# An mLSTM and dilated attention block: the chunk products as fp32r matmuls of high and low parts, with the state as a pair

## What is computed

```python
def step(carry, inp):
    C, n, m = carry
    k_j, v_j, a_j, bt_j = inp
    m_new = jnp.maximum(bt_j + m, a_j.max(-1))
    decay = jnp.exp(bt_j + m - m_new)
    w = jnp.exp(a_j - m_new[..., None])
    C_new = decay[..., None, None] * C + jnp.einsum('bhl,bhlk,bhlv->bhkv', w, k_j, v_j)
    n_new = decay[..., None] * n + jnp.einsum('bhl,bhlk->bhk', w, k_j)
    return (C_new, n_new, m_new), (C, n, m)
...
s = jnp.einsum('bhnld,bhnsd->bhnls', qc, kc) * jnp.exp(log_d - m_t[..., None])
num = inter[..., None] * jnp.einsum('bhnld,bhndv->bhnlv', qc, C_prev) + jnp.einsum('bhnls,bhnsv->bhnlv', s, vc)
den = inter * jnp.einsum('bhnld,bhnd->bhnl', qc, n_prev) + s.sum(-1)
h = num / jnp.maximum(jnp.abs(den), jnp.exp(-m_t))[..., None]
```

## Time and profile before

| | us |
|---|---|
| median of 3 runs | 1372.53 (1372.0 to 1373.92) |
| the profiled execution, its own time | 1374.74 |
| its span, first to last instruction | 1372.9 |
| busy in the span: PE / DVE / ACT / POOL | 1352.4 / 792.1 / 642.1 / 568.1 |
| PE's chain share of the span | 89% |
| granted PE clock, mean | 0.996 of 2.4 GHz |

### The profile page before, as it was taken

How to read it: one execution, slowest core, us unless ns; L and a number is a source line. 1 busy time by engine, 2 the same in 40 slices (tenths; PEclk the granted TensorE clock), 3 DMA queues, 4 the chain that set the end, 5 groups by cost and what they waited for, 6 DMA issues and landing times.

```text
span 1372.9 us, 18735 instructions
## 1 busy us (share of the span) xinstructions
PE 1352.4 (99%) x6448; PEld 1126.6 (82%) x6448; DVE 792.1 (58%) x1261; ACT 642.1 (47%) x1320; POOL 568.1 (41%) x399
## 2 busy tenths in 40 slices
PE   7999999999999999999999999999999999999998
PEld 4788888888888888888888888888888888788786
DVE  4864338245543835877657675755644442897632
ACT  5644543553454455445545455444544553533421
POOL 3353435335443534664434445344343554454000
PEclk8999999999999999999999999999999999999999
DMA  6123233324333232454442635345343354966421
...
DMA packets 210462, 165.02 MB, mean 120 GB/s; under 512 B 32400, under 2 KB 186544, under 8 KB 210368
## 3 DMA queue, kind: packets, MB, share of 16 engines
...
...
q10 hardware_dynamic: 432, 0.10, 0.0%
...
## 4 chain that ended last, share of the span: by engine, by line
PE 89%; DVE 4%; DMA 2%; issue 2%; ACT 2%; SPq 1%; POOL 0%; ACTq 0%; DVEq 0%; POOLq 0%
PE proj L1240 68%; PE side L1185 3%; PE proj L1185 2%; PE side L1285 2%; PE side L1264 2%; PE side L1341 2%; PE side L1350 2%; PE side L1273 1%; PE side L1313 1%; PE side L1346 1%; DMA hm_raw_T<-hm_spill 1%; PE proj L1166 1%; PE side L1166 1%; PE side L1296 1%; PE side L1358 1%
## 5 line engine op out<-in xcount | busy, mean ns | idle before, releaser
L1075 POOL TENSOR_TENSOR w_lo<-raw,w_hi 128x512 fp32r<-128x512 f32 x161 | 233.3, 1450 | 410.7 <-ACT w_hi L1449 410.7
L1240 PE MATMUL proj<-hi_T,w_hi 128*128 128x512 f32 x832 | 338.2, 406 | 2.3 <-ACT snap L1467 1.6
L1240 PE MATMUL proj<-hi_T,w_lo 128*128 128x512 f32 x832 | 325.2, 391 | 0.0
L1240 PE MATMUL proj<-lo_T,w_hi 128*128 128x512 f32 x832 | 324.1, 390 | 0.0
L1240 PE MATMUL proj<-hi_B,w_hi 128*128 128x512 f32 x624 | 255.0, 409 | 5.5 <-ACT b_sb L1511 5.5
L1240 PE MATMUL proj<-hi_B,w_lo 128*128 128x512 f32 x624 | 245.0, 393 | 0.0
L1240 PE MATMUL proj<-lo_B,w_hi 128*128 128x512 f32 x624 | 244.6, 392 | 0.0
L1075 POOL TENSOR_TENSOR w_lo<-s_sb,w_hi 128x512 fp32r<-128x512 f32 x104 | 157.0, 1513 | 156.9 <-ACT w_hi L1449 156.8
L1240 PEld LDWEIGHTS proj<-hi_T,w_hi 128*128 128x128 f32 x832 | 156.4, 188 | 36.3 <-issue 3.7
L1240 PEld LDWEIGHTS proj<-hi_T,w_lo 128*128 128x128 f32 x832 | 156.1, 188 | 34.2
L1240 PEld LDWEIGHTS proj<-lo_T,w_hi 128*128 128x128 f32 x832 | 156.6, 188 | 30.3
...
## 6 DMA issues: line engine op xcount, KB each, us to landing
...
```

The lines of the kernel that those rows point to most:

```text
L1075: TT(w_lo_ring[k % RING][:], src, w_hi_ring[k % RING][:].bitcast(F32), ALU.subtract).then_inc(lo_pool, 1)
L1240: mm = pe.matmul(acc(p, which), w[:, kt, :], m[:, kt, :], start=(first and kt == 0 and w is wh and m is h_hi[b]), stop=(kt == 3 and w is w ...
```

## The change

The scores stay as they are. All other products of the chunks become three fp32r matmuls each, of a high and a low part (`three_products`). That needs:

- on ACT, vv and kw written as fp32r high parts (vv_hi, kw_hi), and a new copy q_hi of the chunk's q (not in a head's first chunk);
- on DVE, at a chunk's start: vv_lo and kw_lo from PSUM less the high parts, ahead of the product of scores and mask, which now goes in place into dmat; a cast cw_hi and a subtraction cw_lo of it; and q_lo, which is written over q in the chunk's buffer;
- on DVE, at a chunk's end: the state as a pair state_hi and state_lo. The two halves from PSUM are added to the decayed state_lo into state_sum, then the decayed state_hi is added (128x516), and the sum is cast into state_hi and the rest written into state_lo;
- single buffers for vv, kw, w and the gate of o, where there were two. ACT waits for the last product of the chunk before (L1715 before: of the one two back), and the gate's tanh for the gating of the chunk before;
- PE's end of a chunk waits for kv_done (now DVE's), q_low, st_done and w_done;
- apart from this, the second load of x counts on the semaphore of the first one (x_in) in place of one of its own.

```diff
@@ -470,11 +470,17 @@
             pos[0] += (int(np.prod(shape[1:])) * size + 31) // 32 * 32
             return t
 
-        state = small("state", [P, 2, VE], F32)
-        kw_sb = [small(f"kw{i}", [P, MD], F32) for i in range(2)]
-        vv_sb = [small(f"vv{i}", [P, VE], F32) for i in range(2)]
-        w_sb = [small(f"w{i}", [P, P], F32) for i in range(2)]
-        o_gate = [small(f"o_gate{i}", [P, MD], F32) for i in range(2)]
+
+        state_hi = small("state_hi", [P, 2, VE], F32R)
+        state_sum = small("state_sum", [P, 2, VE], F32)
+
+        state_lo = at("state_lo", [P, 2, VE], F32R, pos[0] - (2 * VE * 4 + 31) // 32 * 32)
+        q_hi = at("q_hi", [P, 2, P], F32R, A_P + 26112)
+        q_lo = [at(f"q_lo{i}", [P, 2, P], F32R, A_P + 16896 + i * 4608) for i in range(2)]
+        kw_hi, kw_lo = small("kw_hi", [P, MD], F32R), small("kw_lo", [P, MD], F32R)
+        vv_hi, vv_lo = small("vv_hi", [P, VE], F32R), small("vv_lo", [P, VE], F32R)
+        cw_hi, cw_lo = small("cw_hi", [P, P], F32R), small("cw_lo", [P, P], F32R)
+        o_gate = small("o_gate", [P, MD], F32)
         dmat = small("dmat", [P, P], F32)
         total = small("total", [P, VE], F32)
         sq_junk = small("sq_junk", [P, MD], BF16, 2)
...
@@ -1330,25 +1338,33 @@
                     mm = pe.transpose(keep[:, MD + d * P:MD + (d + 1) * P], cb_[:, 4 + d, :], ident[:])
                 mm.then_inc(pe_keep, 1)
 
+            def three_products(into, w, m):
+
+                for i, (a, b) in enumerate(((0, 0), (0, 1), (1, 0))):
+                    mm = pe.matmul(into, w[a], m[b], start=(i == 0), stop=(i == 2))
+                return mm
+
             def chunk_end(h, n):
                 c = chunk_no(h, n)
-                v = vv_sb[c % 2][:]
+                v = (vv_hi[:], vv_lo[:])
                 pe.wait_ge(kv_done, c + 1)
                 pe.wait_ge(ones_done, 1)
                 if n:
-                    ring_taken(pe, ("C", h, n - 1, 1))
+                    pe.wait_ge(q_low, later_no(h, n))
+                    pe.wait_ge(st_done, later_no(h, n))
                     for d in range(2):
-                        mm = pe.matmul(keep[:, 0:VE], chunk_sb[c % 2][:, d, :], state[:, d, :],
-                                       start=(d == 0), stop=(d == 1))
+                        for a, m in ((q_hi, state_hi), (q_hi, state_lo), (q_lo[c % 2], state_hi)):
+                            mm = pe.matmul(keep[:, 0:VE], a[:, d, :], m[:, d, :], start=(d == 0 and a is q_hi and m is state_hi),
+                                           stop=(d == 1 and a is not q_hi))
                     mm.then_inc(pe_keep, 1)
-                ring_taken(pe, ("qk", h, n))
+                pe.wait_ge(w_done, c + 1)
                 b = work(("B", h, n))
-                pe.matmul(b[:, 0:VE], w_sb[c % 2][:], v, start=True, stop=True).then_inc(pe_ring, 1)
+                three_products(b[:, 0:VE], (cw_hi[:], cw_lo[:]), v).then_inc(pe_ring, 1)
                 if n < NT - 1:
                     for d in range(2):
                         b = work(("C", h, n, d))
-                        pe.matmul(b[:, 0:VE], kw_sb[c % 2][:, d * P:(d + 1) * P], v, start=True, stop=True
-                                  ).then_inc(pe_ring, 1)
+                        keys = slice(d * P, (d + 1) * P)
+                        three_products(b[:, 0:VE], (kw_hi[:, keys], kw_lo[:, keys]), v).then_inc(pe_ring, 1)
 
             def head_output(h, f):
                 d, j2 = f // 2, f % 2
@@ -1711,18 +1727,25 @@
                             act.wait_ge(cols_exp, 1)
                             act.wait_ge(att_out, 16 * AH)
                         act.wait_ge(pe_keep, keep_no["kv", h, n] + 1)
-                        if c > 1:
-                            act.wait_ge(pe_ring, ring_no[last_use(*divmod(c - 2, NT))] + 1)
-                        ins = A(vv_sb[c % 2][:, 0:MD], keep[:, MD:2 * MD], ACT.Copy)
+                        if c:
+                            act.wait_ge(pe_ring, ring_no[last_use(*divmod(c - 1, NT))] + 1)
+                        ins = A(vv_hi[:, 0:MD], keep[:, MD:2 * MD], ACT.Copy)
                         if n < NT - 1:
-                            ins = A(kw_sb[c % 2][:], keep[:, 0:MD], ACT.Copy, scale=cols[:, 2, h, n:n + 1])
-                        ins.then_inc(kv_done, 1)
+                            ins = A(kw_hi[:], keep[:, 0:MD], ACT.Copy, scale=cols[:, 2, h, n:n + 1])
+                        ins.then_inc(kv_hi, 1)
+                        if n:
+
+                            if later_no(h, n) > 1:
+                                hp, n2 = (h, n - 1) if n > 1 else (h - 1, NT - 1)
+                                act.wait_ge(pe_keep, keep_no["A", hp, n2] + 1)
+                            act.wait_ge(chunk_in[c % 2], 32 * (c // 2 + 1))
+                            A(q_hi[:], chunk_sb[c % 2][:, 0:2, :], ACT.Copy).then_inc(q_high, 1)
                         act.wait_ge(d_done, c + 1)
                         A(dmat[:], dmat[:], ACT.Exp, bias=cols[:, 0, h, n:n + 1]).then_inc(e_done, 1)
                         act.wait_ge(pe_ring, ring_no["oT", h, n] + 1)
-                        if c > 1:
-                            act.wait_ge(chunk_ready, c - 1)
-                        A(o_gate[c % 2][:], bank[ring_no["oT", h, n] % BANKS][:, 0:MD], ACT.Tanh, scale=0.5
+                        if c:
+                            act.wait_ge(chunk_ready, c)
+                        A(o_gate[:], bank[ring_no["oT", h, n] % BANKS][:, 0:MD], ACT.Tanh, scale=0.5
                           ).then_inc(ring_act, 1)
                     elif what == "end":
                         h, n = it[1:]
@@ -2151,18 +2174,29 @@
                 if c == 0:
                     dve.wait_ge(att_out, 16 * AH)
                     dve.wait_ge(dec_in, 16)
-                    step(V.memset(vv_sb[0][:, MD:VE], 1.0))
-                    V.memset(vv_sb[1][:, MD:VE], 1.0).then_inc(ones_done, 1)
+                    step(V.memset(vv_hi[:, MD:VE].bitcast(F32), 1.0))
+                    V.memset(vv_lo[:, MD:VE].bitcast(F32), 0.0).then_inc(ones_done, 1)
                 else:
-                    ring_taken(dve, ("qk", *divmod(c - 1, NT)))
+                    dve.wait_ge(w_done, c)
                 dve.wait_ge(chunk_in[c % 2], 32 * (c // 2 + 1))
                 TT(dmat[:], neg_g[c % 2][:], tril[:], ALU.add).then_inc(d_done, 1)
+                dve.wait_ge(kv_hi, c + 1)
+                ins = TT(vv_lo[:, 0:MD], keep[:, MD:2 * MD], vv_hi[:, 0:MD].bitcast(F32), ALU.subtract)
+                if n < NT - 1:
+                    ins = STT(kw_lo[:], keep[:, 0:MD], cols[:, 2, h, n:n + 1], kw_hi[:].bitcast(F32), ALU.mult, ALU.subtract)
+                ins.then_inc(kv_done, 1)
                 i = ring_no["qk", h, n]
                 dve.wait_ge(pe_ring, i + 1)
-                if c > 1:
-                    dve.wait_ge(pe_ring, ring_no["B", (c - 2) // NT, (c - 2) % NT] + 1)
                 dve.wait_ge(e_done, c + 1)
-                TT(w_sb[c % 2][:], bank[i % BANKS][:, 0:P], dmat[:], ALU.mult).then_inc(ring_dve, 1)
+                TT(dmat[:], bank[i % BANKS][:, 0:P], dmat[:], ALU.mult).then_inc(ring_dve, 1)
+                ring_taken(dve, ("qk", h, n))
+                if c:
+                    dve.wait_ge(pe_ring, ring_no["B", *divmod(c - 1, NT)] + 1)
+                step(V.tensor_copy(cw_hi[:], dmat[:]))
+                TT(cw_lo[:], dmat[:], cw_hi[:].bitcast(F32), ALU.subtract).then_inc(w_done, 1)
+                if n:
+                    dve.wait_ge(q_high, later_no(h, n))
+                    TT(q_lo[c % 2][:], chunk_sb[c % 2][:, 0:2, :], q_hi[:].bitcast(F32), ALU.subtract).then_inc(q_low, 1)
 
             def chunk_end(h, n):
                 c = chunk_no(h, n)
@@ -2180,17 +2214,25 @@
                 if c >= HM_SLOTS:
                     hp, n2 = divmod(c - HM_SLOTS, NT)
                     dve.wait_ge(pe_ring, ring_no["hmT", hp, 2 + n2 // 4] + 1)
-                STT(hm_slot(h, n), o_gate[c % 2][:], 1.0, total[:, 0:MD], ALU.add, ALU.mult).then_inc(chunk_ready, 1)
+                STT(hm_slot(h, n), o_gate[:], 1.0, total[:, 0:MD], ALU.add, ALU.mult).then_inc(chunk_ready, 1)
                 if n < NT - 1:
+                    if chunk_no(h, n) - h:
+                        dve.wait_ge(st_done, chunk_no(h, n) - h)
                     for d in range(2):
                         i = ring_no["C", h, n, d]
                         dve.wait_ge(pe_ring, i + 1)
                         part = bank[i % BANKS][:, 0:VE]
                         if n:
-                            STT(state[:, d, :], state[:, d, :], decay[:, h, n:n + 1], part, ALU.mult, ALU.add
+                            STT(state_sum[:, d, :], state_lo[:, d, :].bitcast(F32), decay[:, h, n:n + 1], part, ALU.mult, ALU.add
                                 ).then_inc(ring_dve, 1)
                         else:
-                            V.tensor_copy(state[:, d, :], part).then_inc(ring_dve, 1)
```

(9 more changed lines are left out.)

8 lines of the change are left out of this document (5 added, 3 removed).

## The result

| | before | after |
|---|---|---|
| median of 4 runs each, us | 1373.22 (1372.0 to 1374.43) | 1397.78 (1396.55 to 1398.89) |
| ratio, 95% interval | | 1.0176 [1.0164, 1.0187] |
| the profiled execution, its span, us | 1372.9 | 1394.8 |
| granted PE clock, mean | 0.996 | 0.993 |

A forecast was written before the change was run, and what follows sets the result against it. PE was taken to bound the kernel, busy for 437.0 of 437.0 us in the chunks. -10.4 us on PE and +15.5 of waits for DVE made +5.1, so 1377.5 us on the median, range 1363 to 1387.

The forecast's parts named there:

- PE's part: Chunks' products on PE: 432 fp32r matmuls at 0.121 us replace 288 fp32 instructions at 0.2175; 10.4 us less.
- Rival 4: On PE, weight loads don't hide behind matmuls of 258 columns and set the pace: some 1405 us; chance 0.03.
- The mechanism: DVE's added work makes PE wait for q_lo and at turns of o, in heads 0 to 2, none in head 3.
- the term of 15.5 us for DVE's delay: PE's waits on late DVE work in the heads' chunks, added to the forecast as 15.5 us.
- The prediction's own walk: DVE's and ACT's queues followed instruction by instruction; PE waits 17 us in four places in heads 0 to 2.
- a reason that no row shows: For taking 15.5 us rather than 17: a first wait of PE also spaces the rows behind it.
- start group: DVE's additions at a chunk's start (vv_lo, kw_lo, cast and subtraction for cw, q_lo), charged 0.3 us for POOL.
- end group: DVE's additions at a chunk's end (128x516 update, cast, subtraction for the state pair), charged 0.3 us for POOL.
- the charge for POOL: DVE instructions reading two SBUF tensors are held by POOL: 0.3 us per new group of a chunk, between 0 and 0.5.
- the prediction's own four sums: PE's waits: 11.6 us without POOL's charge, 17 with 0.3, 23.4 with 0.5, 22 with slow cast and 0.3.
- the slow cast: DVE's state cast at its upper end of 0.65 us instead of 0.30; with POOL's 0.3, PE waits 22 us.
- Rival 3: Worse contention: DVE holds POOL, weights come late, the cast is slow; waits of 26 us or more, from 1388; chance 0.05.

The follow-up runs named there:

- no_qlo: The changed kernel without DVE's q_lo; PE makes the same 432 matmuls with q_hi in its place, low part of q left out: 1384.75 us, 1.0078 of the kernel before.
- state_one: The changed kernel without the state's low part, state_hi updated straight from PSUM, q_lo kept, 432 matmuls kept: 1370.04 us, 0.9976 of the kernel before.
- after_notaps: The changed kernel with two of the convolution's three taps left out on DVE: 1369.02 us, 0.9967 of the kernel before; that kernel without these taps took 1373.05.

## Why the prediction was right, and where it went wrong

**PE's part was right.** 0.1195 us per matmul against 0.121, 11.0 us against 10.4. Rival 4, a weight load that sets the pace, did not come: there is one load and one matmul every 0.12 us. The Trainium skill, "TensorE: Matmul & The Clock Gate", under what overlaps and what doesn't, says that a load overlaps a matmul only in another row group. The trace does not agree with it at 258 columns either.

**The mechanism was right.** PE waits for q_lo, and at the turn of o, and in head 3's time only 1.0 us, for another instruction of DVE. Chunks 1 and 2 lose a little over 5 us where 3.8 were walked, and 1.7 of these are the clock. The split was off: 1.94 us for q_lo and 0.93 for the turn of o, where 1.1 and 2.5 were walked. DVE's busy time in the stretch came to 385.21 (380 to 395 forecast). PE waits for neither POOL nor SP there, and for ACT 1.4 us for `total` and 1.1 for snap.

**The step that failed is the term of 15.5 us for DVE's delay.** By PE's rows 28.6 us of waiting stand in its place, and 5.1 us of slow clock for which the sum had no term; by the medians 35.6 were lost. The prediction's own walk summed to 17, and was taken down to 15.5 for a reason that no row shows. Its parts:

| | predicted | measured |
|---|---|---|
| POOL's hold and slower pieces, start group, us per chunk | 0.3 | 0.87 |
| POOL's hold, end group (without the cast) | 0.3 | 0.16 |
| cast of the state, us each | 0.30 | 0.43 least, 0.50 mean |
| losses in head 0 | 8.9 | 10.3 |
| in head 1 | 3.1 | 11.7 |
| in head 2 | 5.3 | 12.0 |
| clock at 1.2 GHz | 0 | 5.1 (1.7 in each of these) |

Without the clock head 0 lost 8.6 us, as walked; heads 1 and 2 lost 10.0 and 10.3 and not 3.1 and 5.3. There five of seven q_lo are held, in head 0 three.

*First, the charge for POOL.* It was put at 0.3 us in the middle of a range up to 0.5, and it was 0.87 for the start's group: q_lo (1159 ns, 0.42 by itself) 0.74 and cw_lo (414, 0.29) 0.13. The step that gave it was wrong in kind. It took the mean hold of the gating as that of any instruction, as if POOL's work fell anywhere. But the place of a new instruction in the queue fixes what it meets: 19 of 28 q_lo met a w_lo for nearly its whole length. An estimate from the prediction's own four sums (11.6, 17 and 23.4 us for a charge of 0, 0.3 and 0.5, and 5 more for the slow cast) makes some 27 us of the measured prices, a mean charge of 0.52 and a cast of 0.50. That is near the 28.6 measured. But it is not the whole answer. In no_qlo, with q_lo and its hold both gone, those sums would give under 14.5 us, and PE is idle for 15.2 with 3.4 of slow clock on top. So the walk itself reads low too, and how the loss parts between the charge and the walk's small slack in heads 1 and 2 stays open. The experiments give the price of a crowded queue directly: taking away 32 us of DVE's busy time (no_qlo) gives back 13, some 56 (state_one) 28, some 42 (after_notaps) 29, that is 0.4 to 0.7 us for each us. The mean idle time of 165 us in the earlier trace rows told nothing of that.

*Second, a term for the clock was missing.* The forecast has PE's gaps at 1 to 3 us and nothing of what follows them. Behind three of them the clock costs 5.1 us more.

Waits and clock together are 33.7 us by PE's rows. The 35.6 of the medians are some 2 us more; that lies within what separates a profiled execution from a median here, and was not followed. The cast took 0.43 us by itself and 0.50 in the mean, between its two ends of 0.30 and 0.65. The cycle table of the Trainium skill, "VectorE: DVE Perf Modes", would make it 0.33 by the estimate in the prediction; the trace shows 0.43 at least, and the trace decides.

**The range was too narrow**, since its upper end came from 0.5 us per group and the slow cast apart, not from both together with a term for the clock. Rival 3 from 1388 on was given 0.05. It is near to what came out in its number, but not in its reason: PE waited for no weights and for POOL in no row of these heads.
